# Attention scores as three rounded products over half of the array's rows

## What is computed

```python
ATTN_GROUPS = ((128, 1), (512, 4), (2048, 16))     # window, dilation
HEADS_PER_GROUP, HEAD_DIM, BLOCK = 8, 64, 128
...
    def with_prev(t):
        prev = jnp.pad(t, ((0, 0), (1, 0), (0, 0), (0, 0), (0, 0)))[:, :-1]
        return jnp.concatenate([prev, t], axis=2)
    qb = to_blocks(q)
    kc = with_prev(to_blocks(k))
    vc = with_prev(to_blocks(v))
...
    logits = jnp.einsum('nbqhd,nbkhd->nbhqk', qb, kc) + bias
    logits = jnp.where(mask[None, :, None], logits, -jnp.inf)
    m = jnp.max(logits, axis=-1, keepdims=True)
    p = jnp.exp(logits - m)
    den = jnp.sum(p, axis=-1)
    o = jnp.einsum('nbhqk,nbkhd->nbqhd', p, vc) / jnp.transpose(den, (0, 1, 3, 2))[..., None]
```

## Time and profile before

| | |
|---|---|
| median of three runs | 4841.41 us |
| span of the profiled execution | 4842.2 us |
| attention stage in it | about 1400 to 1788 us |
| TensorE busy, products | 4696.1 us, 97% of the span |
| VectorE busy | 2756.4 us, 57% |
| ScalarE busy | 1916.7 us, 40% |
| GpSimd busy | 700.9 us, 14% |
| mean granted TensorE clock | 0.984 |

### The profile page before, as it was taken

How to read it: one execution, slowest core, us unless ns; L and a number is a source line. 1 busy time by engine, 2 the same in 40 slices (tenths; PEclk the granted TensorE clock), 3 DMA queues, 4 the chain that set the end, 5 groups by cost and what they waited for, 6 DMA issues and landing times.

```text
span 4842.2 us, 75558 instructions
## 1 busy us (share of the span) xinstructions
PE 4696.1 (97%) x26332; PEld 4107.6 (85%) x26332; DVE 2756.4 (57%) x5732; ACT 1916.7 (40%) x3152; POOL 700.9 (14%) x783
## 2 busy tenths in 40 slices
PE   8999999999889999999699999999999999999998
PEld 7888888788679987787699999999988888999997
DVE  4343333111356678555456556566667777778887
ACT  4212112111136672233233334344445555556665
POOL 0000000232212101123101111111011111111121
PEclk9999999999999999999799999999999999999999
DMA  4322222322454345543445555656566566677777
GB/s 140 111 70 80 73 80 83 117 88 89 153 183 145 128 169 184 174 139 122 164 161 156 196 186 183 201 170 213 181 225 215 208 237 231 230 244 273 275 265 257
DMA packets 262082, 823.24 MB, mean 170 GB/s; under 512 B 39273, under 2 KB 70804, under 8 KB 224341
## 3 DMA queue, kind: packets, MB, share of 16 engines
q1 hardware_dynamic: 228728, 715.02, 41.0%
q0 software_dynamic: 28304, 88.03, 7.8%
q10 hardware_dynamic: 4829, 17.31, 1.0%
HBM read 661.67 MB, written 163.88 MB: 170 GB/s over the span
## 4 chain that ended last, share of the span: by engine, by line
PE 50%; DMA 0%; DVE 0%; ACT 0%; issue 0%; POOL 0%; SPq 0%; ACTq 0%; DVEq 0%; POOLq 0%
PE ex_d L2445 14%; PE ex_g L2412 11%; PE ex_g L2414 9%; PE ex_g L2408 7%; PE ex_d L2408 4%; PE ex_d L2439 3%; PE ex_d L2414 2%; PE ex_g L2389 1%; DMA ex_bd<-in_b_down 0%; PE ex_d L2389 0%; PE ex_d L2420 0%; DMA ex_xg<-h_d,ex_nxt 0%; ACT ex_wgh L2487 0%; DVE ex_x L2599 0%; ACT ex_x L2500 0%
## 5 line engine op out<-in xcount | busy, mean ns | idle before, releaser
L2414 PE MATMUL ex_g<-ex_x,ex_wgl 128*128 128x256 f32 (+12 forms) x3456 | 986.8, 286 | 0.0
L2412 PE MATMUL ex_g<-ex_x,ex_wgh 128*128 128x288 f32 (+5 forms) x3584 | 763.2, 305 | 12.4 <-DVE ex_biases L2691 12.4
L2414 PEld LDWEIGHTS ex_g<-ex_x,ex_wgl 128*128 128x128 f32 x3456 | 655.2, 190 | 4.3
L2581 DVE TENSOR_TENSOR ex_wgl<-ex_wg,ex_wgh 128x2048 fp32r<-128x2048 f32 x274 | 626.8, 2288 | 41.8 <-ACT ex_wgh L2487 41.7
L2487 ACT ACTIVATE ex_wgh<-ex_wg 128x2048 fp32r<-128x2048 f32 x274 | 523.7, 1911 | 305.4 <-PE ex_g L2414 278.2
L2412 PEld LDWEIGHTS ex_g<-ex_x,ex_wgh 128*128 128x128 f32 x3584 | 597.5, 189 | 21.6 <-issue 12.8
L2408 PE MATMUL ex_g<-ex_x,ex_wgh 128*128 128x512 f32 (+6 forms) x1664 | 529.7, 376 | 0.9 <-DVE ex_t L2611 0.9
L493 PE MATMUL prj_p<-prj_wh,prj_hh 128*128 128x512 f32 x1280 | 501.0, 391 | 1.4 <-DVE prj_hl L620 1.4
L493 PE MATMUL prj_p<-prj_wh,prj_hl 128*128 128x512 f32 x1280 | 499.5, 390 | 0.0
L493 PE MATMUL prj_p<-prj_wl,prj_hh 128*128 128x512 f32 x1280 | 499.5, 390 | 0.0
L2445 PE MATMUL ex_d<-ex_wdh,ex_ath 128*128 128x512 f32 x992 | 400.4, 404 | 1.1 <-DVE ex_ath L2639 1.1
(11 more groups left out here) (429 smaller groups left out, 8794.3 us busy)
## 6 DMA issues: line engine op xcount, KB each, us to landing
ex_wg<-in_w_gu SPq DMA_DIRECT2D x276, 1024.0 KB, 5.2
ex_wd<-in_w_down SPq DMA_DIRECT2D x276, 512.0 KB, 6.5
qkv_d<-prj_o SPq DMA_DIRECT2D x144, 256.0 KB, 2.0
wo_spare<-qkv_d SPq DMA_DIRECT2D x40, 768.0 KB, 4.3
prj_raw<-in_w_in SPq DMA_DIRECT2D x109, 256.0 KB, 3.3
ex_bd<-in_b_down SPq DMA_DIRECT2D x34, 512.0 KB, 8.6
gate_d<-prj_o SPq DMA_DIRECT2D x64, 256.0 KB, 2.0
mix_ring<-gate_d SPq DMA_DIRECT2D x32, 512.0 KB, 4.3
```

Of the source, the lines that this page charges most:

```text
L2412: pe.matmul(out[:, 0:size], h[:, k, j, :], x[:, k, 0:size], start=(k == 0 and x is xh), stop=False)
L2414: last = pe.matmul(out[:, 0:size], l[:, k, j, :], xh[:, k, 0:size], start=False, stop=(k == KD - 1))
L2581: tt(flat(wgl[z][:, :, :, :]), flat(wg[r][:, :, :, :]), flat(wgh[z][:, :, :, :]).bitcast(F32), ALU.subtract).then_inc(wgl_ready, 1)
```

## The change

The scores are formed as three rounded products. q and k are each split into a part rounded to float32r (`qh`, `kh`) and the rest (`ql`, `kl`), and the score of a head is qh kh + qh kl + ql kh, accumulated in PSUM. Each product uses only the 64 partitions of its head, so the zero-padded `qz` is gone, and heads e = 0 and e = 1 alternate. Each of the two heads writes to a PSUM bank of its own: four score banks in two pairs instead of three, and one bank for turned probabilities instead of two. The waits on those buffers move up by one unit.

The high parts are written by ScalarE (`save_q` one copy, `save_k` new, with the gain as scale, after unit j = 2), the low parts by VectorE (`save_q` new, in step j = 1, `save_k` now in step j = 3). GpSimd copies the carried half of both `kh` and `kl`, and no longer clears anything.

```diff
-        qz = [t_.sb(f"qz{z}", [P, HG, P]) for z in range(2)]
-        kT = [t_.sb(f"kT{z}", [P, NFT, 2 * P]) for z in range(2)]
+        qh, ql = ([t_.sb(f"{n}{z}", [P, NFT, P], F32R) for z in range(2)] for n in ("qh", "ql"))
+        kh, kl = ([t_.sb(f"{n}{z}", [P, NFT, 2 * P], F32R) for z in range(2)] for n in ("kh", "kl"))
...
-        sb = [t_.ps(f"s{z}", (P, 2, 2 * P)) for z in range(3)]
-        tb = [t_.ps(f"t{z}", (P, 2, 2 * P)) for z in range(2)]
+        sb = [[t_.ps(f"s{z}{e}") for e in range(2)] for z in range(2)]
+        tb = t_.ps("t", (P, 2, 2 * P))
...
+        def scores_at(u, e, off):
+
+            return sb[u % 2][e][:, off:2 * P]
...
             @block.gpsimd
             def _(pool):
-                for z in range(2):
-                    pool.memset(qz[z][:, :, :], 0.0).then_inc(zeros, 1)
                 t_.clear_used(pool)
                 for n in range(NBL):
                     if goes_on(n + 1):
-                        pool.wait_ge(k_ready, n + 1)
+                        pool.wait_ge(kl_ready, n + 1)
                         if n:
                             pool.wait_ge(s_mm, PB * n)
-                        pool.tensor_copy(kT[(n + 1) % 2][:, :, 0:P], kT[n % 2][:, :, P:2 * P]).then_inc(k_kept, 1)
+                        for t in (kh, kl):
+                            pool.tensor_copy(t[(n + 1) % 2][:, :, 0:P], t[n % 2][:, :, P:2 * P]).then_inc(k_kept, 1)
...
                 def turn_q(n):
...
-                        pe.wait_ge(k_ready, n)
+                        pe.wait_ge(kl_ready, n)
...
                 def turn_k(n):
-                    pe.wait_ge(q_ready, 2 * n + 2)
+                    pe.wait_ge(ql_ready, n + 1)
...
                     if j == 0:
-                        pe.wait_ge(k_ready, n + 1)
+                        pe.wait_ge(kl_ready, n + 1)
                         if not off:
-                            pe.wait_ge(k_kept, kept[n])
-                    if u >= 3:
-                        pe.wait_ge(s_read, 2 * (u - 3) + 2)
-                    for e in range(2):
-                        last = pe.matmul(sb[u % 3][:, e, off:], qz[n % 2][:, 2 * j + e, :], kT[n % 2][:, j, off:],
-                                         start=True, stop=True)
+                            pe.wait_ge(k_kept, 2 * kept[n])
+                    if u >= 2:
+                        pe.wait_ge(s_read, 2 * (u - 2) + 2)
+                    z = n % 2
+                    for q, k in ((qh, kh), (qh, kl), (ql, kh)):
+                        for e in range(2):
+                            rows = slice(DH * e, DH * e + DH)
+                            last = pe.matmul(scores_at(u, e, off), q[z][rows, j, :], k[z][rows, j, off:],
+                                             start=(q is qh and k is kh), stop=(q is ql))
                     last.then_inc(s_mm, 1)
 
                 def turn_p(u):
                     n = u // PB
                     pe.wait_ge(p_ready, 2 * u + 2)
-                    if u >= 2:
-                        pe.wait_ge(pt_ready, u - 1)
+                    if u:
+                        pe.wait_ge(pt_ready, u)
...
                 def save_q(n):
                     act.wait_ge(q_turned, n + 1)
-                    for e in range(2):
-                        rows = slice(DH * e, DH * e + DH)
-                        act.activation(qz[n % 2][rows, e:HG:2, :], qk[rows, :, :], ACT.Copy).then_inc(q_ready, 1)
+                    act.activation(qh[n % 2][:, :, :], qk[:, :, :], ACT.Copy).then_inc(qh_ready, 1)
+
+                def save_k(n):
+                    g = blocks[n][0]
+                    act.wait_ge(k_turned, n + 1)
+                    act.activation(kh[n % 2][:, :, P:2 * P], qk[:, :, :], ACT.Copy, scale=gains[1][:, g:g + 1]).then_inc(kh_ready, 1)
...
                     if j == 0 and n + 1 < NBL:
                         save_q(n + 1)
+                    if j == 2 and n + 1 < NBL:
+                        save_k(n + 1)
...
+                def save_q(n):
+                    dve.wait_ge(qh_ready, n + 1)
+                    dve.tensor_tensor(ql[n % 2][:, :, :], qk[:, :, :], qh[n % 2][:, :, :].bitcast(F32),
+                                      ALU.subtract).then_inc(ql_ready, 1)
+
                 def save_k(n):
                     g = blocks[n][0]
-                    dve.wait_ge(k_turned, n + 1)
-                    dve.tensor_scalar(kT[n % 2][:, :, P:2 * P], qk[:, :, :], gains[1][:, g:g + 1], None,
-                                      ALU.mult).then_inc(k_ready, 1)
+                    dve.wait_ge(kh_ready, n + 1)
+                    dve.scalar_tensor_tensor(kl[n % 2][:, :, P:2 * P], qk[:, :, :], gains[1][:, g:g + 1],
+                                             kh[n % 2][:, :, P:2 * P].bitcast(F32), ALU.mult,
+                                             ALU.subtract).then_inc(kl_ready, 1)
...
                     if step < NU:
                         add_bias(step)
-                    if j == 2 and n + 1 < NBL:
+                    if j == 1 and n + 1 < NBL:
+                        save_q(n + 1)
+                    if j == 3 and n + 1 < NBL:
                         save_k(n + 1)
                     if step >= 2:
                         save_p(step - 2)
```

More of the change, by code:

```diff
@@ L1202, in attention @@
         bias_in = [t_.sem(f"bias_in{g}") for g in range(len(GROUPS))]
-        (y0_in, gain_ready, high, low, zeros, q_turned, q_ready, k_turned, k_ready, k_kept, s_mm, s_read, p_ready, t_mm, pt_ready, pv_mm,
-         o_saved) = t_.sems("y0_in gain_ready high low zeros q_turned q_ready k_turned k_ready k_kept s_mm s_read p_ready t_mm "
-                            "pt_ready pv_mm o_saved")
+        (y0_in, gain_ready, high, low, q_turned, qh_ready, ql_ready, k_turned, kh_ready, kl_ready, k_kept, s_mm, s_read, p_ready,
+         t_mm, pt_ready, pv_mm, o_saved) = t_.sems(
+            "y0_in gain_ready high low q_turned qh_ready ql_ready k_turned kh_ready kl_ready k_kept s_mm s_read p_ready "
+            "t_mm pt_ready pv_mm o_saved")
+        def scores_at(u, e, off):
+            return sb[u % 2][e][:, off:2 * P]
         def first(n):
@@ L1304, in turn_p @@
                     pe.wait_ge(p_ready, 2 * u + 2)
-                    if u >= 2:
-                        pe.wait_ge(pt_ready, u - 1)
+                    if u:
+                        pe.wait_ge(pt_ready, u)
                     for e in range(2):
                         for k in range(first(n) // P, 2):
-                            last = pe.transpose(tb[u % 2][:, e, k * P:(k + 1) * P], pp[u % 3][:, e, k * P:(k + 1) * P],
+                            last = pe.transpose(tb[:, e, k * P:(k + 1) * P], pp[u % 3][:, e, k * P:(k + 1) * P],
                                                 ident[:, :])
@@ L1343, in _ @@
             def _(act):
-                act.wait_ge(zeros, 2)
                 def save_q(n):
                     act.wait_ge(q_turned, n + 1)
-                    for e in range(2):
-                        rows = slice(DH * e, DH * e + DH)
-                        act.activation(qz[n % 2][rows, e:HG:2, :], qk[rows, :, :], ACT.Copy).then_inc(q_ready, 1)
+                    act.activation(qh[n % 2][:, :, :], qk[:, :, :], ACT.Copy).then_inc(qh_ready, 1)
[3 more added lines that the diff above has]
+                    act.activation(kh[n % 2][:, :, P:2 * P], qk[:, :, :], ACT.Copy, scale=gains[1][:, g:g + 1]).then_inc(kh_ready, 1)
                 def probabilities(u):
@@ L1368, in _ @@
                 save_q(0)
+                act.wait_ge(gain_ready, 1)
+                save_k(0)
                 for u in range(NU):
@@ L1401, in add_bias @@
                         h = 2 * j + e
-                        dve.tensor_tensor_reduce(sc[u % 3][:, e, off:], sb[u % 3][:, e, off:],
+                        dve.tensor_tensor_reduce(sc[u % 3][:, e, off:], scores_at(u, e, off),
                                                  bias[blocks[n][0]][:, h, off:], 1.0, MASKED, ALU.add, ALU.min,
@@ L1410, in save_p @@
                         dve.wait_ge(pv_mm, u - 2)
-                    dve.tensor_copy(ppT[u % 3][:, :, off:], tb[u % 2][:, :, off:]).then_inc(pt_ready, 1)
+                    dve.tensor_copy(ppT[u % 3][:, :, off:], tb[:, :, off:]).then_inc(pt_ready, 1)
+                save_q(0)
                 save_k(0)
```

## The result

| kernel | median us (lowest to highest, runs) | ratio to before, 95% interval | profiled span |
|---|---|---|---|
| before | 4841.41 (4837.71 to 4844.16, 21) | | 4842.2 |
| after | 4849.71 (4844.26 to 4855.98, 21) | 1.0015 (1.0009 to 1.0021) | 4845.4 |

The account below looks back on a forecast made before the run. TensorE was taken to bound the attention stage. Full blocks -0.64 x 27 = -17.3, half blocks +0.99 x 20 = +19.8 and the last +0.3 made +2.8 on 4841.4, so 4844.2 us; 8-in-10 range 4826 to 4907.

Parts of the forecast that it names:

- Time of a product: In the scores, one rounded product takes 0.117 us at 256 columns and 0.107, its weight load, at 128.
- Two heads side by side: In the scores, both heads' half-row products overlap, making three pairs instead of six products, records 13 ns apart.
- Change of tiling: Around each step's scores, entering costs 0.09 us idle plus 0.107 load, and leaving costs 0.15.
- rival C: At the scores, tiling changes cost no idle array and hide their load; each step 0.29 us less, 4808 us; chance 0.09.
- Wait for k's low part: The next block's first scores wait for k's subtraction: 0.18 us in a full block, 0.58 in a half one.
- Wait for q's low part in the half block: The k turn waits 0.10 us for q's low part in a half block, nothing in a full one.
- Single bank for T: Transposing probabilities into one buffer instead of two costs nothing; without cover, 0.1 or 0.2 us a step.
- Start of the stage: The split chain before the first block is one copy and one subtraction longer; taken as zero with GpSimd's copies and clears.
- rival D: In half blocks, waits drop the clock to 1.2 GHz; 16 half blocks cost +85 us, about 4929; chance 0.04.
- GpSimd's copies: Copying two carried halves adds 0.6 us a block, with a whole block until needed; taken as zero.
- Each half block: A half block goes from 5.55 to 6.54 us, +0.99, times 20 is +19.8.
- B: In the scores, the two row tiles do not overlap; each step 0.32 to 0.34 us more, 4907 us; chance 0.14.

Follow-up runs that it names:

- k_early: The changed kernel with both steps of k's split one unit earlier, ahead of that unit's probabilities and bias; 4834.15 us, 0.9983 of before.
- bursts128: two_bursts with all six score products over all 128 rows, heads not separated; 5033.13 us, 1.0395 of before.
- k_early_fill: k_early with identity transposes added where TensorE waits in the first two blocks; 4831.21 us, 0.9978 of before.
- two_bursts: The changed kernel with each step's scores split in two, turns and probability transposes between, so four tiling changes a step; 5225.30 us, 1.0792 of before.
- again: The changed kernel with no edit, run and profiled once more; 4847.11 us, 1.0012 of before.
- high_only: The changed kernel with only the high product left, two score products a step instead of six; 4876.18 us, 1.0065 of before.
- high_rows128: high_only with its two products over all 128 rows, heads not separated; 4815.89 us, 0.9950 of before.
- pairs: k_early with scores of two units back to back, 96 ways in and out of the tiling instead of 192; 4838.29 us, 0.9993 of before.
- in_turn: The changed kernel with three score products of head 0, then three of head 1, instead of alternating; 4851.28 us, 1.0030 of before.
- warm: The changed kernel with thirteen identity transposes before the first k turn and first scores; 4851.28 us, 1.0020 of before.

## Why the prediction was right, step by step

- **Time of a product (0.117, 0.107):** right. Pairs 0.12 apart in the full block, 0.11 in the half one (1749.52 to 1749.63), as far as the second and third pair.
- **Two heads side by side:** right, and closer than thought: 3 to 4 ns between the records of a pair instead of 13.
- **Change of tiling, 0.09 + 0.107 in, 0.15 out:** right. V takes 0.94 until S starts (1445.91 to 1446.85) where T and V together left it 0.84 (1.28 less 0.44): 0.10 of idle. S's first pair is 0.22 ahead of the second, a pitch and a load. From the last pair to T it is 0.205, a pitch and 0.09, and T takes 0.05 more: 0.14 on the way out. Together 0.35 a step as foreseen; a full step was put at 1.99 and took 1.98. The Trainium skill's page "TensorEngine Tiling (Array Packing)", section "Key Properties", says that a change of mode drains the engine; the trace agrees, and rival C, a free change, falls.
- **Wait for k's low part, 0.18 and 0.58:** right, shown by k_early (0.19 and 0.58).
- **Wait for q's low part in the half block, 0.10:** too large. The subtraction is of two operands and took 0.69 where 0.75 was taken for both; the half block of k_early, without the wait for k, is 5.88 against 5.86 of TensorE's own, and the k turn starts 0.04 later behind the last pair (0.25) than a T that waits for nothing (0.21). The 0.06 less and four offsets of 0.01 account for the 0.08 by which the half blocks were shorter than foreseen (they would give 0.10), and the offsets for 0.04 of the 0.06 in the full ones.
- **Single bank for T, zero:** right for this order: 0.5 us in the stage. bursts128 shows what it costs when the order takes the cover away.
- **Start of the stage, zero:** the term that failed most. It cost 5.3 us of blocks 0 and 1. The prediction took the longer split chain there as hidden and did not ask the question of rival D where TensorE has the most waits: the first S waited 1.62 for k and the k turn of block 1 waited 0.57 for q's low part, all at a clock that had not yet come up, and it came up 12 to 16 us later than before. k_early_fill, with the gaps filled, brings back 4.2 against k_early. Waits alone don't explain it, since before waits as long there. Nor do the tiles: the clock was at half for 10.2 us before, for 17.1 to 23.9 in the three runs whose products are rounded but over 128 rows, for 23.9 to 27.3 with 64-row tiles and no fills (in two_bursts for the whole stage). Whether it is the rounded products or where the waits lie, no run here separates.
- **GpSimd's copies, zero:** wrong, and before had the wait already. They do not have "a whole block": the program gives GpSimd its work in one order, and a piece of weights (a wait of 13.8 us for its load in again, then 3.4 to split it) can stand ahead of them. In the first profile of after this cost little (1.12 ahead of block 21, where about 0.5 is usual behind a half block); in high_only, high_rows128, k_early_fill and pairs it cost more. No run here puts the copies ahead of the split.
- **Each half block, +0.99:** the steady ones of group 2 went up by 0.91. In group 1, where a half block stands between full ones, it and the full one behind it went from 14.98 to 15.62, 0.64 where the sum has 0.35.
- **From profile to median:** the forecast carried the difference of two profiles over to the medians. The profiled execution of before had a wait of 2.03 for GpSimd and a fall of the clock behind it, that of after a wait of 1.12 and no fall, and the medians ended 5.1 further apart than the profiles.
- **Sums:** 0.82 stands for four steps where the text has 4 x 0.20. B's S in a half block is 0.84 by its own terms, not 0.80, and C's step 0.35 less, not 0.29; that moves B up by about 3 us and C down by about 10, and no chance rests on it.
- **Rival D** was rightly unlikely for this kernel and right as a mechanism: in_turn shows it in its half blocks (4.05 each, where D had 5.3), high_only in its full ones. Its counter-argument, that a stretch with 84% busy had kept the clock, carried less than it seemed: that was other work in another stage.

## What to carry to other kernels

Two products over 64 rows each run side by side and pay, but each burst of them costs about 0.35 us to get in and out of that tiling (0.10 idle, 0.107 of load, 0.14 out): make the bursts long, and count the price per burst and not per product, since under 256 columns it can be more than the halved products give. A split into a high and a low part adds a subtraction to the chain that feeds the next block; put it in front of the work that isn't needed next, which here was worth 13 us. Treat every wait of half a microsecond in a stage like this as a risk to TensorE's clock, the more where it has half-row bursts, and look at the granted clock of the first blocks and of several runs before trusting one profile. And before putting a wait down to the engine that a view names, look at when that engine was done: here GpSimd's copies of 0.6 us each, stuck behind work for a later stage, released several of the longest waits.

## What the runs showed of the hardware

- With 64-row tiles changing against 128-row work, the clock stayed at 1.2 GHz while TensorE was busy in the records without a gap: 105.00 of 105 us in high_only, 80.00 of 80 in in_turn, 297.30 of 300 in two_bursts. Over 128 rows high_only's products kept it at 0.98 while busy 94.67 of 105. But it is not the tiles alone: in bursts128, all over 128 rows, it stayed at 1.2 GHz for 191.1 us with TensorE busy 164.22 of 170.
- It fell behind waits of 0.5 to 1.1 us (0.52 in in_turn, 0.93 in again, 1.01 in high_only, 1.11 in warm), and elsewhere such waits left it alone (0.51 at 1751.18 and 1.12 at 1592.40, both in after).
- S(0) waiting for GpSimd's copy started 0.10 us behind the copy's end, each time; behind VectorE's subtraction it was 0.05 (1751.13 to 1751.18).
- Two row tiles are fed independently of each other: products that stand three places apart in the program start 10 ns apart.
